# Pooling layer: GpSimd makes the whole low tiles of the fourth to eighth input tile, VectorE none of them

## The reference, cut to what matters

```python
def _pool_mixer(h, w_in, w_grp, scale, w_out):
    bsz, length, _ = h.shape
    z = (h @ w_in).astype(jnp.float32).reshape(bsz, length, POOL_GROUPS, POOL_GROUP_DIM)
    cs = jnp.concatenate([jnp.zeros_like(z[:, :1]), jnp.cumsum(z, axis=1)], axis=1)
    ...
    pooled = (cs[:, hi, gidx] - cs[:, lo, gidx]) / cnt - z
    y = jnp.einsum('blgc,gcd->blgd', pooled, w_grp.astype(jnp.float32)).reshape(bsz, length, POOL_WIDTH)
    y = (y * scale.astype(jnp.float32)).astype(h.dtype)
    return y @ w_out
```

## Time and profile before

| | us |
|---|---|
| median of 3 runs | 1925.36 (1922.24 to 1926.13) |
| the profiled execution | 1926.24 |
| its span in the trace | 1924.4 |
| PE, PEld, DVE, ACT, POOL busy | 1891.0, 1694.0, 1527.0, 924.4, 407.0 |
| pooling layer, first input product to first output product | 1029.66 to 1068.76 |

### The profile page before, as it was taken

One profiled execution on the slowest core, in us unless ns is written; L12 is line 12 of the kernel. 1 busy time (PEld: TensorE's weight loads), 2 busy tenths in 40 slices (PEclk: granted clock), 3 DMA queues, 4 the chain that ended last, 5 costly groups with the idle time before them and its releaser, 6 DMA issues.

```text
span 1924.4 us, 38569 instructions
## 1 busy us (share of the span) xinstructions
PE 1891.0 (98%) x13356; PEld 1694.0 (88%) x13356; DVE 1527.0 (79%) x2601; ACT 924.4 (48%) x1484; POOL 407.0 (21%) x205
## 2 busy tenths in 40 slices
PE   6999999999999999999999999999999999999998
PEld 6999999998888888888889899999888878888887
DVE  6876599957998888888886569994898888886555
ACT  3464444545555544444445444454555544444444
POOL 1544468820000000000003358870000000000000
PEclk8999999999999999999999999999999999999999
DMA  8855445555544445478883345455554454545553
GB/s 320 323 200 204 137 166 181 178 184 208 208 174 168 172 173 174 174 269 320 323 299 121 110 165 175 175 185 188 206 209 166 171 174 172 172 173 191 190 194 131
DMA packets 104182, 376.43 MB, mean 196 GB/s; under 512 B 12464, under 2 KB 12464, under 8 KB 103856
## 3 DMA queue, kind: packets, MB, share of 16 engines
q1 hardware_dynamic: 103680, 373.43, 54.6%
q0 software_dynamic: 432, 2.10, 0.3%
HBM read 374.43 MB, written 1.05 MB: 195 GB/s over the span
## 4 chain that ended last, share of the span: by engine, by line
PE 55%; issue 18%; POOL 15%; DMA 4%; DVE 4%; ACT 2%; SPq 1%; POOLq 0%; DVEq 0%; ACTq 0%
PE O L1530 12%; PE O L1532 12%; PE O L1531 12%; POOL wL L405 9%; PE ring L1496 7%; POOL wL L392 6%; PE ring L1498 4%; DMA raw<-in_u 3%; PE ring L1240 2%; PE ring L1241 2%; PE ring L1242 2%; ACT wH L434 2%; DVE wL L691 2%; PE ring L1472 2%; PE O L1472 1%
## 5 line engine op out<-in xcount | busy, mean ns | idle before, releaser
L434 ACT ACTIVATE wH<-raw 128x1024 fp32r<-128x1024 f32 x608 | 645.0, 1061 | 915.5 <-DMA raw<-in_v 376.8
L691 DVE TENSOR_TENSOR wL<-raw,wH 128x1024 fp32r<-128x1024 f32 x416 | 509.4, 1225 | 238.1 <-ACT wH L434 232.2
L1240 PE MATMUL ring<-hX,wH 128*128 128x256 f32 x1512 | 433.0, 286 | 5.3 <-DVE wL L679 3.8
L1241 PE MATMUL ring<-hX,wH 128*128 128x256 f32 x1512 | 427.6, 283 | 0.0
L1242 PE MATMUL ring<-hX,wL 128*128 128x256 f32 x1512 | 427.6, 283 | 0.0
L1530 PE MATMUL O<-wH,gateH 128*128 128x512 f32 x1024 | 406.5, 397 | 0.8 <-DVE gateL L1122 0.4
L1532 PE MATMUL O<-wH,gateL 128*128 128x512 f32 x1024 | 400.0, 391 | 0.0
L1531 PE MATMUL O<-wL,gateH 128*128 128x512 f32 x1024 | 398.8, 389 | 0.0
L1496 PE MATMUL ring<-hX,wH 128*128 128x512 f32 x1024 | 367.5, 401 | 0.0
L1240 PEld LDWEIGHTS ring<-hX,wH 128*128 128x128 f32 x1512 | 289.8, 192 | 7.6 <-POOL wL L405 2.7
L1241 PEld LDWEIGHTS ring<-hX,wH 128*128 128x128 f32 x1512 | 290.0, 192 | 0.1
(11 more groups left out here) (177 smaller groups left out, 2167.7 us busy)
## 6 DMA issues: line engine op xcount, KB each, us to landing
raw<-in_u SPq DMA_DIRECT2D x256, 512.0 KB, 3.4
raw<-in_v SPq DMA_DIRECT2D x256, 512.0 KB, 3.5
ada_v<-in_ada SPq DMA_DIRECT2D x40, 512.0 KB, 4.9
raw<-in_w_in SPq DMA_DIRECT2D x32, 512.0 KB, 4.4
raw<-in_w_q SPq DMA_DIRECT2D x32, 512.0 KB, 3.5
ada_s<-in_ada SPq DMA_DIRECT2D x20, 512.0 KB, 5.1
ada_f<-in_ada SPq DMA_DIRECT2D x16, 512.0 KB, 11.1
raw<-in_w_out SPq DMA_DIRECT2D x16, 512.0 KB, 3.5
```

Of the source, the lines that this page charges most:

```text
L434: nc.scalar.activation(wH[s % RAW][:, :], raw[s % RAW][:, :], ACT.Copy).then_inc(s_h, 1)
L691: nc.vector.tensor_tensor(wL[s % RAW][:, :], raw[s % RAW][:, :], wH[s % RAW][:, :].bitcast(fp32), ALU.subtract).then_inc(s_low, 1)
L1240: mm(bank[:, 0:T], a, xH[:, k0 + k, :], start=(first and k == 0), stop=False)
L1241: mm(bank[:, 0:T], a, xL[:, k0 + k, :], start=False, stop=False)
```

## The change

GpSimd makes the whole low part of tiles 3 to 7 of the pooling layer's input weights, where it made the second half; VectorE no longer makes their first half. `p_out` 0 and 1 keep their shared form. TensorE waits for one semaphore ahead of each of the five tiles, `s_low_p`, where it waited for `s_l0` and, in the middle, for `s_l1`. The counts are mended: the low instruction of `p_out` 0 raises `s_l0` and `s_l1` by 6 on each engine, and the numbers from which the second search stage counts are moved by 5. The first turns of GpSimd's loop are written out. Nothing is changed on ScalarE and SyncE.

```diff
         HALVES = (0, BASE["p_in", 1] - BASE["u", 0])
-        BY_POOL = (BASE["u", 0], BASE["u", 1] - SEARCH)
+        BY_POOL = (BASE["u", 0], BASE["u", 1] - SEARCH - 5, BASE["p_in", 1] - SEARCH + 3)
...
                     low_second(0, 0, 2, 3)
                     low_second(0, 0, 3)
-                with pool.Fori(1 - layer, (end - base) // 4) as i:
+                else:
+                    for s in range(3):
+                        low_second(base, 0, s)
+                    for j in range(3, KT):
+                        low_whole(base, j // 4, j % 4)
+                    low_second(base, 2, 0, 6)
+                    for s in range(1, 4):
+                        low_second(base, 2, s)
+                with pool.Fori((1, 3)[layer], (end - base) // 4) as i:
                     for s in range(4):
                         low_second(base, i, s)
...
                     for j in range(1, KT):
-                        ahead(base, j // 4, j % 4)
+                        if j > 5:
+                            low_first(base, j // 4, j % 4 + 2, 6 if j == 6 else 1)
                         if j == 4:
                             modulations(7, (8, 9, 10), O[3], (3,))
                         if j in (3, 5, 7):
...
                         if j > 2:
                             pe.wait_ge(s_bank_v, KT + j + 1)
-                            tile_product(BASE["p_in", 1], j // 4, j % 4, ring[j % 4], hH, hL)
+                            tile_product(BASE["p_in", 1], j // 4, j % 4, ring[j % 4], hH, hL, by_pool=2)
```

## The result

The changed kernel took 1932.27 us (median of 6 runs, 1930.14 to 1937.47), the kernel before, run beside it, 1924.80: ratio 1.0040, 95% interval 1.0028 to 1.0052. That is 7.5 us slower, where 2.2 were forecast, and above the range's end of 1930.8. By the prediction's own bound of 3.9 us this is slower, which had a chance of 0.20. A ratio and its interval are given as recorded; a ratio isn't the quotient of the two medians and differs from it by up to 0.0007.

The account below looks back on a forecast made before the run. TensorE was taken as the bound, busy for 98% of the span, with idle time only in the pooling layer. Terms +3.8, -0.5 and -1.1 gave +2.2 us on the median 1925.36, so 1927.6; range 1923.5 to 1930.8.

Parts of the forecast that it names:

- the prediction's own bound of 3.9 us: Whole-kernel time: about 0.2%, 3.9 us, is what a measurement can tell from no change.
- The deciding property: Pooling layer: GpSimd and VectorE take turns, whichever comes second standing until the first ends; 2.85 us per turn.
- The wait: TensorE ahead of the first group products: new idle stretch until `pool(1)` ends, 3.8 us.
- Rival 2: Pooling layer: VectorE's additions don't stand behind GpSimd's whole tiles; 2.5 us earlier, 1922.9; chance 0.10.
- The sum of the turns: TensorE's path in the pooling layer: +3.8 at `pool(1)`, -0.5 at `pool(3)`, -1.1 behind tile 7, +2.2 us.
- The waits behind tile 7: TensorE ahead of the later group products: 1.6 us of waits left instead of 2.7.
- the forecast: Pooling layer: longer turns delay the last group products by 2.2 us, without a clock term; 1927.6 us; chance 0.48.
- rival 1: TensorE at tile 5: the idle stretch lets its clock fall to half; total +3.7, 1929.1; chance 0.30.

Follow-up runs that it names:

- e4_narrow: Changed kernel with GpSimd's instruction for tiles 3 to 7 covering 128 columns in place of 1024, their low part left out: 1923.67 us, ratio 0.9998.
- e5: Changed kernel with 15 dummy products on TensorE ahead of the first group products and 6 ahead of the last: 1927.01 us, ratio 1.0011.
- e11: Changed kernel with 15 and 6 dummy products on TensorE, a second time: 1927.66 us, ratio 1.0013.
- e12_fill_first: Changed kernel with the 15 dummy products ahead of the first group products alone: ratio 1.0014.
- s3_changed: Changed kernel unaltered, a further profiled execution to count falls of the clock: stage 42.63 us.
- e3_vector: Kernel before, with VectorE making whole low tiles of input tiles 6, 7 and output tiles 0, 1, GpSimd none of these: 1925.16 us, ratio 1.0000.
- e7_vector_fill: Kernel before, with VectorE making whole low tiles of input 6, 7 and output 0, 1, 2, plus five dummies before the last group products: 1922.13 us, ratio 0.9985.
- s2_changed: Changed kernel unaltered, a further profiled execution to count falls of the clock: stage 43.54 us.
- e8_three: The change for tiles 3, 4 and 5 alone (GpSimd whole, VectorE none), tiles 6 and 7 shared as in the kernel before: ratio 1.0006.
- e6_again: Changed kernel unaltered, compared a second time with the kernel before: 1929.61 us, ratio 1.0024.
- e9_again2: Changed kernel unaltered, compared a third time with the kernel before: 1932.40 us, ratio 1.0034.
- s1_changed: Changed kernel unaltered, a further profiled execution to count falls of the clock: stage 42.50 us.
- e10_before: Kernel before, unaltered, run as a kernel of its own to show what the comparison gives for no change: ratio 1.0003.
- e1_fill: Changed kernel with 26 dummy products on TensorE ahead of the first group products and 12 ahead of the last: ratio 1.0024.

## Why the prediction was wrong, point by point

**The deciding property: right.** Turns of 2.85 us were forecast; 2.71 to 2.80 were measured. `pool(1)` was to end 26.5 us behind the first input product, and the first group products started at 26.35, 26.26 and 26.09 in the three profiles of the timed comparisons. The wait was forecast at 3.8 us and was 3.45 to 3.57 in the six profiles. e4_narrow shows the cause rather than argues it. Rival 2 (no standing behind whole tiles) is out.

**The sum of the turns: right.** Forecast +2.2 us; with the clock held up the stage was 40.7 us in both profiles (e5, and e11 without the low clock at its start) against 38.8 to 39.1 in the three of the kernel before taken the same way, so +1.7; by the median times of e5 and e11 +2.0 and +1.9.

**The waits behind tile 7: sized somewhat low.** 1.6 us were left there by my count; e5's stage left 1.9 (dummies and the 0.37 behind them) and the changed kernel 2.27. I let the first step of `pool(7)` stand 0.3 us behind GpSimd's half for `p_out` 2; in the profile it took 1.62 instead of 0.72, so 0.9: GpSimd's half ran from 1065.62, and the step started at 1065.84.

**The choice between the forecast and rival 1: this is the step that failed.** I had named the fall of the clock with its place and mechanism, and gave it 0.30 against 0.48. What I set against it, that modulation products and tile 5 end right before at full clock, was no argument: work ahead of an idle stretch of 3.5 us doesn't shorten it. So the forecast's sum has no term for the clock. The runs showed one: a fall in six of six profiles, five times behind the stretch of 3.5 us, and the stage with that fall was 42.4 to 42.6 us in four profiles where it was 40.7 with the clock held up. The Trainium skill (TensorE: Matmul & The Clock Gate, "Why this matters for your kernels") advises against such gaps; by that rule rival 1 was the forecast. The traces agree for five of the six stretches of 3.45 to 3.57 us; and of ten stretches of 2.2 to 2.4 us in all profiles, shorter than those it names, four had a fall behind them.

**Its price: right by the profiles, too low by the times.** Rival 1 counted one stretch and 1.5 us on top, +3.7 in all. In the four profiles with one fall behind the first stretch the stage was 42.5 us, against 41.0 in e12_fill_first (taken without the low clock at its start), which kept the second stretch idle: 1.5 more, and 3.5 more than the kernel before. Once a second fall came at the end, which I had left out. By the median times the changed kernel is 6.2 us dearer (mean of 7.5, 4.6 and 6.6), of which 2.0 are the turns, which leaves 4.3 for the clock and whatever else differs; the two direct comparisons with the dummies give 2.6 and 4.7.

**What stays open.** The profiles account for 4.3 us of the 6.2: from the first input product to the first product behind the norm the changed kernel took 76.6 us on average and the kernel before 72.3. The other two us are not located, but the timed runs say of what kind they are. The mean granted clock was 0.9893 in the 29 runs of the changed kernel (1930.8 us on average), 0.9910 in 116 of the kernel before (1925.0) and 0.9906 in the 23 of e5 and e11 (1927.4). The 0.0017 between the first two is 3.3 us of clock. Among runs with a clock of 0.990 or 0.991 the changed kernel was 3.5 and 2.8 us slower than the kernel before, e5 and e11 1.8 and 2.2. So about half of the excess goes with a lower clock over the whole run, and the dummies take most of that away. This is a relation between means, not a proof: the mean also counts low clock in which TensorE has nothing to do. In which stretches the slower runs lost it no trace shows; no profile of the changed kernel lies above 1931.3 us, and the runs reach 1937.5. The length of the low stretch in the norm behind the layer (3.4 us in most profiles, 6.8 in the first of the changed kernel, in s3_changed and in e5_fill15) is one candidate; it came with and without the cause studied here.

## What to carry to other kernels

Moving the halves from VectorE to GpSimd didn't relieve VectorE, since the two take turns with these instructions (all with two inputs in SBUF). Count the turns: with both lists full each step of a dependent chain cost the other's whole instruction, so put short instructions, or none, beside a chain. An idle stretch of TensorE that a change makes or lengthens beyond those in the trace should be priced with the clock it costs behind it, not by its length alone; dummy products, sized below the stretch, gave 2.6 and 4.7 us back here by the medians. The better way is to not have the stretch. VectorE making whole tiles itself, with GpSimd silent, took two of the three waits away; alone this changed nothing in the time (e3_vector), with one more tile and five dummies in the stretch that was left it was 0.15% faster (e7_vector_fill).

## What the runs showed of the hardware

- The clock fell behind idle stretches of TensorE's weight loads of 2.27, 2.31, 2.28 and 2.38 us (the changed kernel, s2_changed, e8_three, e3_vector). It did not behind six others of 2.21 to 2.38 (e6_again, e9_again2, s1_changed, s3_changed, e12_fill_first, e10_before) nor behind one of 3.55 (s2_changed), so the length alone doesn't decide. Behind those of up to 1.85 us it never did.
- Runs of one kernel differ with the mean granted clock: the kernel before took 1927.9 us on average at 0.989 (12 runs), 1925.0 at 0.991 (29) and 1921.8 at 0.993 (14).
- With both lists full, VectorE and GpSimd took turns, one instruction each: four whole tiles, with a step of `pool(1)` between each two, took 10.83 to 10.85 us in each of the six profiles of the changed kernel, 2.71 us a tile where one alone takes 2.41.
- A dummy product of 128 x 128 in fp32 is two matmuls and costs 0.22 us of TensorE (52 matmuls from 1050.79 to 1056.59 in e1_fill), not the 0.12 I had taken for one.
